# Routed expert layer in fp32: expert jobs ordered one wide, two narrow, with four places for a narrow job's second-layer weights

## What is computed

```python
D_MODEL, SEQ, N_EXPERTS, TOP_K, D_EXPERT = 1024, 1024, 32, 4, 1024

def clamped_swiglu(hcat):
    glu, lin = hcat[..., :D_EXPERT], hcat[..., D_EXPERT:]
    glu = jnp.minimum(glu, 7.0)
    lin = jnp.clip(lin, -7.0, 7.0)
    return glu * jax.nn.sigmoid(1.702 * glu) * (lin + 1.0)

def moe_ffn(h, w_router, b_router, w1, b1, w2, b2):
    t = h.reshape(n, d)                                  # 1024 rows
    logits = (t @ w_router + b_router).astype(jnp.float32)
    top_val, top_idx = lax.top_k(logits, TOP_K)          # 4096 (row, expert) pairs
    top_w = jax.nn.softmax(top_val, axis=-1)
    ...
    def expert_block(args):                              # rows of one expert
        xb, e = args
        act = clamped_swiglu(xb @ w1[e] + b1[e])         # w1[e]: 1024 x 2048
        return act @ w2[e] + b2[e]                       # w2[e]: 1024 x 1024
    ...
    return (weighted sum of the four experts' rows).reshape(b, s, d)
```

## Time and profile before

| | us |
|---|---|
| median of 3 runs | 2728.31 |
| lowest and highest | 2721.39, 2729.66 |
| profiled execution's own time | 2729.92 |
| its span | 2727.6 |

### The profile page before, as it was taken

One profiled execution on the slowest core, in us unless ns is written; L12 is line 12 of the kernel. 1 busy time (PEld: TensorE's weight loads), 2 busy tenths in 40 slices (PEclk: granted clock), 3 DMA queues, 4 the chain that ended last, 5 costly groups with the idle time before them and its releaser, 6 DMA issues.

```text
span 2727.6 us, 44690 instructions
## 1 busy us (share of the span) xinstructions
PE 2582.2 (95%) x15134; PEld 2171.6 (80%) x15135; DVE 1578.5 (58%) x2805; ACT 1144.9 (42%) x1865; POOL 319.1 (12%) x327
## 2 busy tenths in 40 slices
PE   7899988987999997999999999999999999999994
PEld 3356655556888785888888999999999999999994
DVE  5555535676222455777777888884454455445444
ACT  2043424444111334555555766663333333333333
POOL 1000000000000125011111121112112112211211
PEclk9999989999999997999999999999999999999997
DMA  5000010002111374966667788889999999999994
GB/s 146 1 10 6 16 32 16 1 0 63 50 47 51 138 159 110 325 215 215 215 215 215 226 261 262 253 261 303 347 341 340 341 344 338 340 346 335 344 346 156
DMA packets 424967, 527.45 MB, mean 193 GB/s; under 512 B 28116, under 2 KB 334808, under 8 KB 424856
## 3 DMA queue, kind: packets, MB, share of 16 engines
q1 hardware_dynamic: 403816, 464.31, 52.6%
q0 software_dynamic: 20032, 62.11, 9.8%
q10 hardware_dynamic: 1040, 0.00, 0.0%
HBM read 482.23 MB, written 44.14 MB: 193 GB/s over the span
## 4 chain that ended last, share of the span: by engine, by line
PE 58%; DMA 1%; DVE 1%; issue 0%; ACT 0%; POOLq 0%; POOL 0%; SPq 0%; DVEq 0%; ACTq 0%
PE banks L2159 21%; PE banks L2220 17%; PE banks L2171 12%; PE banks L2172 7%; PE banks L2143 1%; DMA acc_rows<-arena,rows 1%; DVE arena L2571 0%; DMA arena<-h_rows,rows 0%; DMA arena<-acc_rows 0%; DVE parts L2427 0%; DVE parts L2410 0%; POOLq L2104 0%; ACT arena L2399 0%; ACT parts L2301 0%; POOL rows L2091 0%
## 5 line engine op out<-in xcount | busy, mean ns | idle before, releaser
L2159 PEld LDWEIGHTS banks<-arena,arena 128*128 128x128 f32 x5376 | 603.5, 192 | 1.6
L2159 PE MATMUL banks<-arena,arena 128*128 128x128 f32 x5376 | 603.6, 275 | 0.0
L2171 PE MATMUL banks<-parts 128*128 128x512 f32 (+1 forms) x1536 | 499.8, 370 | 8.1 <-issue 8.1
L2220 PE MATMUL banks<-parts 128*128 128x512 f32 x2064 | 479.5, 391 | 0.0
L2220 PEld LDWEIGHTS banks<-parts 128*128 128x128 f32 x2064 | 384.2, 188 | 78.8
L2172 PE MATMUL banks<-parts 128*128 128x256 f32 x1536 | 431.2, 281 | 0.0
L2423 DVE TENSOR_TENSOR parts<-arena,parts 128x1024 fp32r<-128x1024 f32 x264 | 314.5, 1221 | 57.7 <-ACT parts L2294 57.3
L2171 PEld LDWEIGHTS banks<-parts 128*128 128x128 f32 x1536 | 289.7, 189 | 45.1 <-issue 8.3
L2172 PEld LDWEIGHTS banks<-parts 128*128 128x128 f32 x1536 | 290.7, 189 | 0.4
L2456 DVE TENSOR_SCALAR arena<-banks,arena 128x128 f32<-128x128 f32 x336 | 101.9, 345 | 317.5 <-PE banks L2159 313.9
L2427 DVE TENSOR_TENSOR parts<-arena,parts 128x1024 fp32r<-128x1024 f32 x192 | 233.5, 1222 | 82.4 <-ACT parts L2301 82.0
(11 more groups left out here) (337 smaller groups left out, 3470.1 us busy)
## 6 DMA issues: line engine op xcount, KB each, us to landing
arena<-in_w SPq DMA_DIRECT2D x264, 1024.0 KB, 7.8
arena<-in_w SPq DMA_DIRECT2D x66, 2048.0 KB, 12.8
arena<-in_x SPq DMA_DIRECT2D x16, 512.0 KB, 9.2
merge_raw<-in_w_in SPq DMA_DIRECT2D x32, 256.0 KB, 2.9
arena<-in_w_in SPq DMA_DIRECT2D x11, 512.0 KB, 5.7
h_rows<-arena POOLq DMA_DIRECT2D x10, 512.0 KB, 8.8
acc_rows<-arena SPq DMA_DIRECT2D x8, 512.0 KB, 6.2
arena<-acc_rows SPq DMA_DIRECT2D x8, 512.0 KB, 7.9
```

The costliest lines, as they stand in the source:

```text
L2159: last = nc.tensor.matmul(bank(g, 2 * (c % 2) + s)[:, a * JOB:a * JOB + P], w1[c][:, s, k, a * P:(a + 1) * P], xt[:, k, 0:P], start=(k == ...
L2171: nc.tensor.matmul(sums[:, :, 0:rows], first_part[p][:, 0, k, :], x_both[:, :, k, 0:rows], start=(k == 0), stop=(k == KT - 1))
L2220: last = nc.tensor.matmul(bank(g, 2 * c + h), x[:, f, h * P:(h + 1) * P], second_part(q, wide)[:, y, a, :], start=(f == 0 and x is act_hi ...
```

## The change

1. **The order.** In the table chain, wide jobs (`code` over 128) are counted (`wides`), and the rank is turned into a place: wide rank r goes to place 3r, narrow ones fill the two places behind each, with limits at both ends. Five steps before the keys go, four come; nine come behind the rank. `job_id` becomes a table of its own, made on GpSimd at the start of the stage, as are three memsets of VectorE's.
2. **Four places.** `narrow_slots` and `piece_used` go. Narrow jobs split pieces 0 to 3 during the first layer (c = 0, 1), and 4 to 7 as wide jobs do, each once PE is through with the piece four before it (`second_free`, on `slot_used`). `slot_used`, `v_hi_ready` and `v_lo_ready` are advanced in narrow jobs so that one count serves both kinds. The low part of the activations of c = 0 is made with that of c = 1 in one step.
3. **A shared end.** Pieces 4 and 5, the next job's input, pieces 6 and 7, the first pieces of a wide next job, and the results are one function `close` behind both kinds on ScalarE and on VectorE. A narrow job can be followed by a wide one and then splits that job's first three pieces.

```diff
@@ stage_out, GpSimd @@
+            pool.iota(g.job_numbers[:, :], pattern=[[1, JOBS]], base=0, channel_multiplier=0).then_inc(ids, 1)
+            for table in (g.job_expert, g.job_place, g.job_count):
+                pool.memset(table[:, JOBS:], 0).then_inc(ids, 1)
+            pool.wait_ge(ids, 11)
...
+            nc.gpsimd.tensor_copy(g.job_ids[:, :], g.job_numbers[:, :]).then_inc(ids, 1)
@@ stage_out, VectorE @@
-            chain.step(nc.vector.tensor_copy(job_id[:, 0:EXPERTS], v.expert_row))
-            chain.step(nc.vector.tensor_scalar(job_id[:, EXPERTS:JOBS], job_e, float(EXPERTS), None, ALU.add))
...
-            for table in (g.job_expert, g.job_place, g.job_count):
-                chain.step(nc.vector.memset(table[:, JOBS:], 0))
...
+            chain.step(nc.vector.tensor_scalar(wide_jobs, code, float(P), None, ALU.is_gt))
+            chain.step(nc.vector.reduce_sum(wides, wide_jobs, AX))
+            chain.step(nc.vector.tensor_scalar(jobs_used, upto[:, EXPERTS - 1:EXPERTS], float(EXPERTS), None, ALU.add))
+            chain.step(nc.vector.tensor_scalar(wides, wides, -0.75, None, ALU.add))
...
             chain.step(nc.vector.reduce_sum(rank_of, before, AX))
-            nc.vector.tensor_scalar(perm, job_id[0:JOBS], rank_of, None, ALU.is_equal).then_inc(keyed.sem, 1)
+            chain.step(nc.vector.tensor_scalar(as_wide, rank_of, jobs_used[0:JOBS], wides[0:JOBS], ALU.add, ALU.subtract))
+            chain.step(nc.vector.scalar_tensor_tensor(out=as_wide, in0=rank_of, scalar=3.0, in1=as_wide, op0=ALU.mult, op1=ALU.min))
+            chain.step(nc.vector.scalar_tensor_tensor(out=as_last, in0=rank_of, scalar=jobs_used[0:JOBS], in1=rank_of, op0=ALU.is_ge, op1=ALU.mult))
+            chain.step(nc.vector.tensor_scalar(as_narrow, rank_of, wides[0:JOBS], 1.5, ALU.subtract, ALU.mult))
...
+            chain.step(nc.vector.tensor_scalar(before, job_id[0:JOBS], as_narrow, None, ALU.is_le))
+            chain.step(nc.vector.tensor_scalar(as_narrow, as_narrow, -1.0, None, ALU.add))
+            nc.vector.scalar_tensor_tensor(out=perm, in0=job_id[0:JOBS], scalar=as_narrow, in1=before, op0=ALU.is_gt, op1=ALU.mult).then_inc(keyed.sem, 1)
@@ stage_experts, PE @@
-                if wide:
-                    pe.sem_inc(piece_used, 2)
+                if not wide:
+                    pe.sem_inc(slot_used.sem, W1_PIECES // 2)
...
-                            elif wide and h == 1:
+                            elif h == halves - 1:
                                 last.then_inc(slot_used.sem, 1)
-                            elif not wide and q < 2:
-                                last.then_inc(piece_used, 1)
@@ stage_experts, ScalarE @@
-                if wide and q >= 4:
+                if q >= 4:
                     second_free(act, n, q - 4)
-                if not wide and q >= 6:
-                    act.wait_ge(piece_used, 2 * n + (q - 5))
...
-                    if not wide and c < 3:
+                    if not wide and c < 2:
                         high(n, 2 * c, False)
                         high(n, 2 * c + 1, False)
...
+            def close(n, count, next_count):
+                for q in range(4, 6):
+                    high(n, q, True)
+                with act.If(next_count > P):
+                    take_x(n + 1, True)
+                with act.Else():
                     take_x(n + 1, False)
                 for q in range(6, 8):
-                    high(n, q, wide)
+                    high(n, q, True)
...
+                with act.Else():
                     next_high()
-                    whole(2)
...
+                    whole(1, False)
@@ stage_experts, VectorE @@
-                        low_act(act_lo[:, fs, 0:P], slice(0, P)).then_inc(act_lo_ready, 1)
-                    if not wide and c < 3:
-                        low(n, 2 * c, False)
-                        low(n, 2 * c + 1, False)
+                        if c == 1:
+                            fs = slice(0, 4)
+                        if c > 0:
+                            low_act(act_lo[:, fs, 0:P], slice(0, P)).then_inc(act_lo_ready, 2 if c == 1 else 1)
+                    if not wide and c < 2:
+                        low(n, 2 * c)
+                        low(n, 2 * c + 1)
+
+            def close(n, count, next_count):
+                for q in range(4, 6):
+                    low(n, q)
+                with dve.If(next_count > P):
+                    take_x(n + 1, True)
+                with dve.Else():
                     take_x(n + 1, False)
                 for q in range(6, 8):
-                    low(n, q, wide)
+                    low(n, q)
...
+                with dve.Else():
+                    whole(1, False)
+                    dve.sem_inc(low_added.sem, 2)
+                next_low()
```

More of the change, by code:

```diff
@@ L1551, in stage_out @@
     keyed = Since(g.row_made, 1)
-    job_id, key, code, place_f = (at(g, ORDER + 64 * n, JOBS) for n in range(4))
+    job_id, key, code, place_f = (g.job_ids[:, :], *(at(g, ORDER + 64 * n, JOBS) for n in range(1, 4)))
     before, perm = at(g, ORDER + 256, JOBS)[0:JOBS], at(g, ORDER + 320, JOBS)[0:JOBS]
@@ L1555, in stage_out @@
     code_of = at(g, ORDER + 448, P)[0:JOBS]
+    wide_jobs = at(g, ORDER + 256, JOBS)
+    wides, jobs_used = (at(g, ORDER + 432 + n, 1) for n in range(2))
+    as_wide, as_narrow, as_last = (at(g, ORDER + 436 + n, 1)[0:JOBS] for n in range(3))
     with nc.Block() as block:
@@ L2219, in second @@
                                 f = 2 * (q % 4) + a
-                                last = nc.tensor.matmul(bank(g, 2 * c + h), x[:, f, h * P:(h + 1) * P], second_part(q, wide)[:, y, a, :],
+                                last = nc.tensor.matmul(bank(g, 2 * c + h), x[:, f, h * P:(h + 1) * P], second_part(q)[:, y, a, :],
                                                         start=(f == 0 and x is act_hi and y == 0), stop=(f == FT - 1 and x is act_hi and y == 1))
@@ L2301, in first_high, with job @@
                 nc.scalar.activation(first_part[p][:, 0], first_of(p), ACT.Copy).then_inc(v_hi_ready.sem, 1)
-            def job(n, wide, count, next_count):
+            def job(n, wide):
                 def split(i):
@@ L2356, in next_high, with whole @@
                         act.nop()
-                def whole(halves):
+                def whole(halves, wide=True):
                     act.wait_ge(yg_free, n + 1)
@@ L2427, in first_low, with job @@
                 nc.vector.tensor_tensor(first_part[p][:, 1], first_of(p), first_part[p][:, 0], ALU.subtract).then_inc(v_lo_ready.sem, 1)
-            def job(n, wide, count, next_count, expert):
+            def job(n, wide, count, expert):
                 def split(i):
@@ L2440, in job @@
                     dve.sem_inc(joined.sem, 8)
+                    dve.sem_inc(v_lo_ready.sem, W1_PIECES)
                 def join(c, s):
@@ L2519, in whole, with add_low @@
                         nc.vector.tensor_scalar(yg[:, h, 0:HALF], bank(g, h), weight(n, h), None, ALU.mult).then_inc(yg_dve, h + 1 if wide else 3)
-                if wide:
+                upper = slice(0, P // 2)
+                def add_low(c):
+                    half = low_sums[:, c * HALF:(c + 1) * HALF]
+                    return nc.vector.tensor_tensor(half, half, bank(g, 1 + 2 * c)[upper], ALU.add)
+                with dve.If(count > P):
                     with dve.If(count > MID):
@@ L2543, in job @@
                         dve.sem_inc(low_added.sem, 1)
-                else:
-                    whole(1)
-                    dve.sem_inc(low_added.sem, 2)
+                    with dve.Else():
+                        dve.nop()
+                with dve.Else():
+                    dve.nop()
             dve.sem_inc(yg_dve, 3)
@@ L2559, in _ @@
                     with dve.If(count > P):
-                        job(n, True, count, next_count, expert)
+                        job(n, True, count, expert)
                     with dve.Else():
-                        job(n, False, count, next_count, expert)
+                        job(n, False, count, expert)
+                    close(n, count, next_count)
                 with dve.Else():
```

79 lines of the change are left out of this document (32 added, 47 removed).

## The result

The changed kernel takes **2783.1 us** (median of 4 runs, 2781.8 to 2786.3) against 2726.8 for the kernel before on the same chip (2721.4 to 2729.7). The ratio is **1.0211, 95% interval 1.0192 to 1.0230**: 56 us slower. The forecast was 2754, some 26 slower, with a range of 2740 to 2770. The direction was right; the size was not.

The account below looks back on a forecast made before the run. PE's own work was taken as the bound, the same in any order. Borders 17, gathers 2.4, table 2.3 and end 3.1 sum to 24.8 us on top: forecast 2754 us (0.9% slower), range 2740 to 2770.

Parts of the forecast that it names:

- Bound and sign: Expert stage: PE's own work bounds it in any order, so mixing job kinds doesn't help; slower was given 0.83.
- Rival (b): Mixing pays: spreading weight loads over the expert stage removes PE's waits of 8.1 and 0.61 us, giving 2719.6; chance 0.07.
- Piece 6: Second layer of a narrow job before a wide one: w2 piece ready at 9.7, wanted at 8.4, stall 1.35 us.
- The start of the wide job: After a narrow job: first piece ready at 12.7, PE through at 12.5, so 0.2 us more at each border.
- The narrow-narrow border: Between two narrow jobs: pieces 6 and 7 ready before wanted, cover 0.9 us, so zero cost for all ten.
- Gathers: Rows gathered after wide jobs: five borders of jobs with 129 to 192 rows wait 0.61 us each, 2.4 more overall.
- The wide job's fourth piece: Wide job after a narrow one: split ready at 19.4, PE wants it at 19.8, so no cost.
- Table and end: Nine added job-table steps on VectorE cost 2.3 us; ending with a wide job costs 3.1 us.
- Rival (c): Instructions fetched at each of 22 kind switches, one or two packets each, PE waiting 1.2 us: 26 more, 2780; chance 0.08.
- Rival (d): Gathers late at all 22 borders between kinds, 1.5 us each in place of 2.4 in all: 2785; chance 0.05.
- The list of what would prove it wrong: Narrow jobs before wide ones no longer than others, those of two narrow neighbours growing, or instruction packets throughout the stage.

## Why the prediction was right in direction and wrong in size

- **Bound and sign: right.** PE was the bound in both regimes, and evening out DMA rate and VectorE's load bought nothing. Rival (b) fell: the regimes were interleaved, and there was no wait of PE for it to remove. The Trainium skill's page Perfetto Trace Analysis (section Optimization Strategy) says that interleaving regimes whose most contended engine differs may bring something; here PE was busy for all of both stretches before, and it brought nothing.
- **Piece 6: right.** 1.35 forecast, 1.24 measured, 11 times, released by the named line; it goes when the input is moved behind the pieces.
- **The start of the wide job: the step that failed.** "PE is through at 12.5: 0.2 more" compared when the data are ready with when PE's matmuls are through. The data came about when I said, but PE's stream had to pass piece 7's wait first and then the loop top. 1.55 to 1.94 of gap in place of 0.2; with the part that the overlap of records hides, the border costs 38.8 in place of 17: 22 of the 31 us by which the account is over the forecast's sum. That the path past the wait sets it, and not the named release, is shown by the load: one more or one less in that path moves the wide job's start by 0.6 to 0.9 us.
- **The narrow-narrow border: the same failure.** "The cover is 0.9 us; I take zero for all ten" gave the cover for the matmuls that read pieces 6 and 7, and that was right. For the loop top piece 7 is wanted 3.2 us before the job's end at 11.1, at 7.9, and it came at 8.5. 0.6 to 0.8 each, 7.1 in all. The two runs of the old order with four places (15 us with the load in the loop top, 2.5 with it moved) show that nothing else is in it.
- **Gathers: right in kind, low in size.** Five borders did wait, those after jobs of 129 to 192 rows, as said, at 0.5 to 0.65 in four of them; the last took 1.34. 3.9 in place of 2.4.
- **The wide job's fourth piece: "Close, but free" held.** PE never waits for it.
- **Table and end: right.** 2.2 and 3.5 for 2.3 and 3.1.
- **Rival (c): its time came near, its cause didn't.** It foretold packets at the switches, and 143 came, about nine for each group of three jobs where it had counted one or two a switch. (Its price of 1.2 us each is also above its own source, which gives 2.0 for two.) But at all eleven narrow-wide borders of the changed kernel no packet starts in the 4 us before the wide job's first matmul, so none lies between piece 7's release and that matmul. Moving one register load takes 0.6 to 0.8 off these gaps and leaves the 143 packets. A wide job of over 192 rows following a narrow one takes no longer (67.2 to 68.0, and 68.85 less the 0.87 of 8 transposes is 67.98 before), and the old order with 47 packets pays the same at its narrow-narrow borders. That its 2780 is so near the measured time is chance: a total close to a rival's doesn't speak for it. Its mechanism may still be there on a small scale, as some gaps that neither a wait nor the loop top explains have a packet that starts up to 3 us before them: the two inside wide jobs of the changed kernel (0.6 in all), five like them (2.2) and the five before narrow jobs (2.4) in the run with the load moved, and the one of the order in two blocks (1.6). No run tests it.
- **Rival (d): no.** Six of the eleven borders after wide jobs don't wait for a gather. Of the narrow jobs before a wide one only the last does, which stands right behind a wide job too.
- The list of what would prove it wrong named "if those of two narrow neighbours grow". They did, by 0.6 to 0.8. It also named packets throughout the stage, and they came.

The account's sum is 55.5 and the medians differ by 56.3, the profiled spans by 52.8; runs of either kernel lie some us apart, and the few us between are not resolved further. No version run here beats the kernel before: the best with the new order is 2762, the best with four places 2730.

## What to carry over

A thing isn't on time because the instruction that reads it doesn't wait. In a loop whose bound engine reads registers and branches at its top, the last wait of an iteration must be over by the length of the loop top before the engine runs dry, so put that time (here 3.2 to 3.5 us on PE) into every cover computed near a loop's end, and move register loads to where the engine's stream is far ahead. And when a wait grows, or two waits become one, look at the granted clock behind it: gaps of 1.98 us brought it down at up to 8 of 11 borders, gaps of at most 1.12 at none.

## What the runs showed of the hardware

- **How far PE's stream runs ahead.** Where nothing holds it, the last register load stands 2.15 to 2.2 us before the first matmul of the job in all borders of the kernel before; where it is held, 1.2 to 1.3 before a narrow job and 1.6 to 1.9 before a wide one. A register load with its register arithmetic is 0.65 to 0.8 us of that (1235.3 to 1236.1 for one to the next), though its own record is 0.30.
- **A gap between PE's records is less than what it costs.** Gaps of 0.43 to 0.51 stood for 0.6 to 0.75 from start to start, since a matmul's end is modelled up to some 0.2 late.
- **The granted clock fell after idle times of 1.98 us** at 8 and 5 of 11 borders, after 2.3 to 2.6 (with 1.24 shortly before) at 6 of 11, after 1.55 to 1.94 (with 1.24 before) at 1 of 11, after at most 1.12 (with 1.24 before) at none. It stayed at 0.50 for 3.4 us at a time and cost 1.5 us. Which of the borders it hits stays open.
- **Fetched code cost little to be seen in the changed kernel**: 97 more packets, none in the 4 us before a wide job that follows a narrow one, and two gaps (0.2 and 0.4) with a packet some 3 us before them. The Trainium skill's page Advanced Engine Details and Errata, section ISA Cache, gives TensorE 128 KB in lines of 16 KB. The packets of the trace agree with the lines (2.34 MB in 143 are 16.4 KB each); the 128 KB no run shows. That the two bodies together don't stay in it would fit the packets; no run here shows their sizes.
- Wide jobs of one size take either 67.2 or 68.0 us within one run (jobs 3 and 6 of the changed kernel) with no gap in them. No run here tells why.
